# Placing the routing weights of eight tokens at once, in front of two expert tiles, in a hybrid mixer and PEER kernel

## The reference

```python
def one_block(xb):
    q = (xb @ w_q).reshape(tb, PEER_HEADS, 2, PEER_KEY_DIM)
    sc = jnp.einsum('thpk,hpnk->thpn', q, sub_keys).astype(jnp.float32)
    s1, i1 = lax.top_k(sc[:, :, 0], PEER_TOPK)
    s2, i2 = lax.top_k(sc[:, :, 1], PEER_TOPK)
    ...
    top_s, pos = lax.top_k(cand, PEER_TOPK)
    idx = jnp.take_along_axis(cidx, pos, axis=-1)
    gw = jax.nn.softmax(top_s, axis=-1).astype(xb.dtype)
    act = jax.nn.gelu(jnp.einsum('td,thkd->thk', xb, u[idx]), approximate=False)
    return jnp.einsum('thk,thkd->td', act * gw, v[idx])
```

## Time and profile before

| | |
|---|---|
| time, median of 3 runs | 1962.33 us (1962.28 to 1962.42) |
| span of the profiled execution | 1961.0 us |
| PE busy, share of the span | 1935.7 us, 99% |
| DVE, ACT, POOL busy | 60%, 49%, 63% |
| the stage of the last 64 up tiles | 217.1 us in each of the two layers |

### The profile page before, as it was taken

The page is one execution under the profiler, slowest core; times in us unless marked ns, Lnnn a source line. Parts: engine busy times, 40 slices in busy tenths (PEclk is TensorE's granted clock), DMA queues, the critical chain, the costliest instruction groups (busy, mean ns, idle before and its releaser), DMA issues.

```text
span 1961.0 us, 39380 instructions
## 1 busy us (share of the span) xinstructions
PE 1935.7 (99%) x13126; PEld 1750.7 (89%) x13126; DVE 1186.3 (60%) x2802; ACT 961.2 (49%) x1521; POOL 1242.2 (63%) x624
## 2 busy tenths in 40 slices
PE   9999999999999999999999999999999999999998
PEld 9888899899999888888898889998999998888886
DVE  4654499368898444444456536983688974444444
ACT  5644445444444444444555544454444444444444
POOL 6446688877776555555474476888777765555553
PEclk9999999999999999999999999999999999999999
DMA  6524555554444666655545245555444445555553
GB/s 217 179 91 145 187 182 176 190 172 156 155 155 156 196 193 192 195 192 194 187 142 185 87 152 186 183 181 189 165 157 152 158 163 192 195 193 193 192 192 135
DMA packets 93245, 338.48 MB, mean 173 GB/s; under 512 B 10353, under 2 KB 10737, under 8 KB 93169
## 3 DMA queue, kind: packets, MB, share of 16 engines
q1 hardware_dynamic: 93168, 337.54, 51.4%
HBM read 336.45 MB, written 1.05 MB: 172 GB/s over the span
## 4 chain that ended last, share of the span: by engine, by line
PE 95%; DVE 2%; ACT 1%; DMA 1%; issue 0%; SPq 0%; DVEq 0%
PE PS L1011 35%; PE PS L934 11%; PE PS L935 10%; PE PS L939 10%; PE PS L896 8%; PE PS L574 6%; PE PS L901 4%; PE PS L948 3%; PE PS L835 2%; DMA ring<-stream 1%; PE PS L559 1%; PE PS L541 1%; PE PS L564 1%; PE PS L560 1%; PE PS L613 1%; PE PS L921 0%
## 5 line engine op out<-in xcount | busy, mean ns | idle before, releaser
L478 POOL TENSOR_TENSOR WL<-ring,WH 128x1024 fp32r<-128x1024 f32 x360 | 867.8, 2412 | 383.0 <-ACT WH L1265 198.4
L1265 ACT CAST WH<-ring 128x1024 fp32r<-128x1024 f32 x512 | 538.2, 1051 | 753.5 <-PE PS L1011 329.7
L508 POOL TENSOR_TENSOR HX<-G,HX 128x256 fp32r<-128x256 f32 x256 | 372.2, 1454 | 320.2 <-ACT HX L1389 320.2
L1938 DVE TENSOR_TENSOR WL<-ring,WH 128x1024 fp32r<-128x1024 f32 x248 | 303.9, 1225 | 370.9 <-ACT WH L1265 370.9
L1011 PE MATMUL PS<-WH,HX 128*128 128x512 f32 x2048 | 506.4, 389 | 0.0
L1011 PEld LDWEIGHTS PS<-WH,HX 128*128 128x128 f32 x2048 | 384.2, 188 | 80.0 <-POOL HX L508 0.5
L934 PE MATMUL PS<-HX,WH 128*128 128x256 f32 x1664 | 418.1, 289 | 0.0
L935 PE MATMUL PS<-HX,WH 128*128 128x256 f32 x1664 | 407.7, 283 | 0.0
L935 PEld LDWEIGHTS PS<-HX,WH 128*128 128x128 f32 x1664 | 319.0, 192 | 0.0
L934 PEld LDWEIGHTS PS<-HX,WH 128*128 128x128 f32 x1664 | 317.9, 191 | 0.0
L1011 PE MATMUL PS<-WL,HX 128*128 128x512 f32 x1024 | 274.0, 389 | 0.0
(11 more groups left out here) (244 smaller groups left out, 1877.6 us busy)
## 6 DMA issues: line engine op xcount, KB each, us to landing
ring<-stream SPq DMA_DIRECT2D x636, 512.0 KB, 3.3
X<-x_t SPq DMA_DIRECT2D x4, 256.0 KB, 3.6
out_t<-X SPq DMA_DIRECT2D x2, 512.0 KB, 2.7
CN<-consts SPq DMA_DIRECT2D x1, 851.0 KB, 9.4
WF<-last SPq DMA_DIRECT2D x1, 512.0 KB, 10.1
PR<-params SPq DMA_DIRECT2D x2, 239.0 KB, 4.5
CN<-consts SPq DMA_DIRECT2D x1, 64.0 KB, 4.0
```

The source lines that it names most:

```text
L478: nc.gpsimd.tensor_tensor(WL[:, b, :], ring[:, slot, :], WH[:, b, :].bitcast(F32), ALU.subtract).then_inc(done, 1)
L508: nc.gpsimd.tensor_tensor(GL[:, s, :], G[:, tile, :], GH[:, s, :].bitcast(F32), ALU.subtract).then_inc(L.gl_ready, 1)
L1265: nc.scalar.copy(WH[:, b, :], ring[:, slot, :]).then_inc(L.hi_ready, 1)
L1938: V.tensor_tensor(WL[:, s % 2, :], ring[:, (U0 + s) % SLOTS, :], WH[:, s % 2, :].bitcast(F32), ALU.subtract).then_inc(L.vlo_ready, 1)
```

## The change

`place` of two groups is run in a row, in front of two up tiles, where each had stood in front of its own tile. The waits of both stand ahead of the first one. Since four groups of one-hots are now alive at once, their slots grow from 8 to 16; the second eight lie in SQ, a tile that has other uses only outside the expert layer. DVE makes four groups of one-hots ahead instead of two, and then runs two `weigh`, two `one_hot` and one `weigh_pair` in turn. ACT's order is as it was.

```diff
-        O2 = OH[:, :, 0:OW]
-        O1 = OH[:, :, OW:OW + 2 * P]
+        OHX = SQ[:, :, :].rearrange("p t n -> p (t n)").bitcast(F16)[:, 0:8 * (OW + 2 * P)].rearrange(
+            "p (s n) -> p s n", s=8)
+        O2 = [OH[:, k, 0:OW] for k in range(8)] + [OHX[:, k, 0:OW] for k in range(8)]
...
                         for i in range(4):
-                            o = bank[6 + g][:, i * P:(i + 1) * P]
+                            o = bank[6 + g % 2][:, i * P:(i + 1) * P]
...
-                    for s in range(SLOTS):
-                        if s % 2 == 0:
-                            pe.wait_ge(L.folded, N_WIDE - 1 + s // 2)
-                        pe.wait_ge(L.o_ready, s + 1)
-                        if s >= 2:
-                            pe.wait_ge(L.w_used, s - 1)
-                        place(s % 2)
-                        experts_in(s, HK + s + 1)
+                    for s in range(0, SLOTS, 2):
+                        pe.wait_ge(L.folded, N_WIDE - 1 + s // 2)
+                        pe.wait_ge(L.o_ready, s + 2)
+                        if s:
+                            pe.wait_ge(L.w_used, s)
+                        for e in range(2):
+                            place(s + e)
+                        for e in range(2):
+                            experts_in(s + e, HK + s + e + 1)
                     with pe.Fori(1, HK // SLOTS) as r:
-                        for s in range(SLOTS):
-                            if s % 2 == 0:
-                                pe.wait_ge(L.gelu_done, r * 2 + (HK // 2 + s // 2 - 1))
-                            pe.wait_ge(L.o_ready, r * SLOTS + (s + 1))
-                            pe.wait_ge(L.w_used, r * SLOTS + (s - 1))
-                            place(s % 2)
-                            experts_in(s, r * SLOTS + (HK + s + 1))
+                        for s in range(0, SLOTS, 2):
+                            pe.wait_ge(L.gelu_done, r * 2 + (HK // 2 + s // 2 - 1))
+                            pe.wait_ge(L.o_ready, r * SLOTS + (s + 2))
+                            pe.wait_ge(L.w_used, r * SLOTS + s)
+                            for e in range(2):
+                                place(s + e)
+                            for e in range(2):
+                                experts_in(s + e, r * SLOTS + (HK + s + e + 1))
...
                     one_hot(0)
+                    one_hot(1)
                     for k in range(SLOTS * TURN_ROUND + 4, SLOTS * TURN_ROUND + 8):
                         fold(k)
-                    one_hot(1)
+                    one_hot(2)
+                    one_hot(3)
...
-                    for g in range(GROUPS):
-                        weigh(g)
-                        if g + 2 < GROUPS:
-                            one_hot(g + 2)
-                        if g % 2 == 1 and g >= 5:
-                            weigh_pair((g - 5) // 2)
+                    for q in range(GROUPS // 2):
+                        weigh(2 * q)
+                        weigh(2 * q + 1)
+                        for g in (2 * q + 4, 2 * q + 5):
+                            if g < GROUPS:
+                                one_hot(g)
+                        if q >= 2:
+                            weigh_pair(q - 2)
```

More of the change, by code:

```diff
@@ L402, in program @@
         i_ps = PS[:, 3, 256:256 + 2 * P].rearrange("p (h e k) -> p e h k", h=HEADS, e=2)
-        O2 = OH[:, :, 0:OW]
-        O1 = OH[:, :, OW:OW + 2 * P]
+        OHX = SQ[:, :, :].rearrange("p t n -> p (t n)").bitcast(F16)[:, 0:8 * (OW + 2 * P)].rearrange(
+            "p (s n) -> p s n", s=8)
+        O2 = [OH[:, k, 0:OW] for k in range(8)] + [OHX[:, k, 0:OW] for k in range(8)]
+        O1 = [OH[:, k, OW:OW + 2 * P] for k in range(8)] + [OHX[:, k, OW:OW + 2 * P] for k in range(8)]
         iota3 = IOB[:, 0:3 * IW].rearrange("p (a b) -> p a b", a=3)
@@ L945, in place @@
                         for i in range(4):
-                            o = bank[6 + g][:, i * P:(i + 1) * P]
+                            o = bank[6 + g % 2][:, i * P:(i + 1) * P]
                             for a in range(2):
-                                mm = nc.tensor.matmul(o, O2[:, 4 * g + i, 0:P], O1[:, 4 * g + i, a * P:(a + 1) * P],
+                                mm = nc.tensor.matmul(o, O2[4 * g + i][:, 0:P], O1[4 * g + i][:, a * P:(a + 1) * P],
                                                       start=(a == 0), stop=(a == 1))
@@ L1875, in one_hot @@
                         for i in range(4):
-                            t, slot = 4 * g + i, g % 2 * 4 + i
-                            V.tensor_scalar(O2[:, slot, 0:3 * IC].rearrange("p (a b) -> p a b", a=3), iota3[:, :, 0:IC],
+                            t, slot = 4 * g + i, g % 4 * 4 + i
+                            V.tensor_scalar(O2[slot][:, 0:3 * IC].rearrange("p (a b) -> p a b", a=3), iota3[:, :, 0:IC],
                                             slotT[:, 1, t:t + 1], None, ALU.is_equal)
                             parts = PS[:, 2 + t // P, 0:2 * P].rearrange("p (a n) -> p a n", a=2)[:, :, t % P]
-                            ins = V.scalar_tensor_tensor(out=O1[:, slot, :].rearrange("p (a n) -> p a n", a=2),
+                            ins = V.scalar_tensor_tensor(out=O1[slot].rearrange("p (a n) -> p a n", a=2),
                                                          in0=bc(iota1, 1, 2), scalar=slotT[:, 0, t:t + 1],
```

## The result

The changed kernel takes 1999.18 us (1998.5 to 1999.67, 5 runs) against 1962.33 (1961.52 to 1962.99, 5 runs): 1.0186 times as long, 95% interval 1.0174 to 1.0197. The forecast was 1999.7, in a range of 1993.5 to 2009.5. The profiled span grew from 1961.0 to 1997.8 us, by 36.8.

A forecast was written before the change was run, and what follows sets the result against it. TensorE, busy for 99% of the span at full clock, was taken to bound the kernel. A wait of +40.9 us and a saving of -3.5 gave 1962.33 + 37.4 = 1999.7 us, range 1993.5 to 2009.5.

The forecast's parts named there:

- The wait: At 62 pair borders TensorE waits for keep(odd): 0.52 + 0.14 us each, 40.9 us in all (36.0 to 47.1).
- The release: From the end of ACT's keep to TensorE's matmul start: 0.14 us taken, with 0.06 and 0.24 as other values.
- the lower bound: Lowest size of the wait at the 62 pair borders: 62 x 0.58 = 36.0 us.
- The saving: Sixteen f16 matmuls in a row halve the changes of kind: 0.055 us per pair, -3.5 us (-4.5 to 0).
- its best pace: Second eight f16 matmuls of a pair at 0.44 us, a little under the mean, which saves 0.07 us.
- The sum: Wait plus saving over the span: +40.9 - 3.5 = +37.4 us, giving 1999.7 us.
- Everything behind the wait moves along: Placings, tiles and other engines' work shift by the same 0.66 us, so the wait returns at every border.
- DVE's order: Costs nothing: one-hots made for the pair after next have a whole pair's cover; without it, 2.3 us per late group.
- The sixteen matmuls kept their pace: Rival: the second eight f16 matmuls go 0.097 us apart, +17 us in place of -3.5, 2020 us; 5%.
- The granted clock was 1.00 in both stages: Rival: pauses lower TensorE's clock, up to +200 us a layer, from 2050 us on; 2%.
- The first rival: keep(odd) ends before the lowers do, so only the saving is left: 1958.8 us, at best 1957.8; 5%.

The follow-up runs named there:

- The wait alone: Kernel before, unpaired, with TensorE waiting in front of an even group for keep of the odd group just before it: 2003.41 us against 1962.52.
- The two parts measured alone: Kernel before with only the later bank wait: 2003.41 us; changed kernel with keep(odd) ahead of the second tile's cast: 1958.29 us; both against 1962.52.
- the 30 borders that were changed: Changed kernel, with one-hot and activation waits moved ahead of the tile before for each loop body's second pair: 1996.65 us against 1962.61.

## Why the prediction was right

- *The wait.* Forecast 62 x (0.52 + 0.14) = 40.9 us. The wait alone measured 2003.41 - 1962.52 = 40.9, and the idle time with its correction gives 41.3. The 0.52, the mean by which `keep` ends too late, was read from rows in which that hurt nobody: the end of `keep` against the start of the *next* placing, which was no wait at the time.
- *The release.* 0.14 us was taken from ACT's other release against 0.06 from DVE's, on the ground that the engines are the same. The size was right and the ground was not: ACT too releases TensorE in 0.05 to 0.06 us, where the bank's wait is the only one at the placing. By the program the matmul of the earlier trace rows also stands behind two waits (the landing of its piece and the emptied bank), which may be why its 0.14 fitted; no run tests that. That the right size came from a wrong ground is luck. With 0.06 the wait would have been the 36.0 us of the lower bound, and the forecast 1994.8.
- *The saving.* Forecast 0.055 us a pair, 3.5 us; measured 0.063 a pair, 4.0 to 4.2 us. This is the one term that was mis-sized, and inside its bounds. The prediction's own working gives 0.51 - 8 x 0.057 = 0.05 us; the 0.055 that it took lies between this and the 0.07 of its best pace, and no row gives it. With the 0.056 of a run of sixteen it is 0.51 - 8 x 0.056 = 0.06, which agrees with the 0.063 as far as starts rounded to 0.01 us can tell.
- *The sum.* The two parts measured alone give 40.9 - 4.2 = 36.7 us; the change itself measured 36.85.
- *Everything behind the wait moves along.* 62 waits at 62 borders show it. Their idle time shrinks from 0.60 to 0.41 us, as the lateness of `keep` in the rows of before does, from 0.62 to 0.41.
- *DVE's order* cost nothing, as forecast. But the reason was half wrong: the prediction said that without the cover of a whole pair, each late group would cost 2.3 us. With eight slots there is no such cover, and still only one border a layer waits, for 0.36 us. DVE makes both groups within the pair; late in the stage it ends 0.18 us before the placing starts.
- *The rivals.* The bank was not free in time. The sixteen matmuls kept their pace. The granted clock was 1.00 in both stages, through 62 pauses of 0.57 to 0.76 us (the idle time with its 0.16).
- *Slips that nothing hangs on.* The weight load of 0.097 us is 0.096 in the earlier trace rows. A pair of the changed kernel lasts 235.28 / 32 = 7.35 us on the mean, where the prediction had some 7.2 in one place and 7.4 in another.

The first rival, that the bank is free in time, named the cure: with `keep` ahead of the cast, the bank is free in time, and the kernel takes 1958.3 us where 1958.8 was worked out.

## What to carry to other kernels

The lesson is drawn from this one kernel. When two steps that alternate between two buffers are joined, the second buffer's wait comes earlier by a whole step. Before joining them, read in the trace when that buffer comes free, although nobody waits for it yet, and see what stands ahead of the freeing instruction on its own engine. If that is work which waits for the end of the present step, move the freeing instruction ahead of it; and let each wait stand only in front of what needs it.

## What was not expected of the hardware

TensorE was released by the same kind of ACT instruction in 0.15 us where the placing had other waits beside that for the bank, though these had long been met, and in 0.05 to 0.06 where it had that one alone. Over the 30 borders that were changed the idle time in brackets fell from 31.4 to 28.8 us, 0.09 us each. The times agree: 1999.18 - 1996.65 = 2.5 us, or 2.8 with each against the kernel before in its own session. The Trainium skill, page "Perfetto Trace Analysis", section "Identifying Dependency Chains", says that an instruction that waits on several engines may have some of its waits put into instructions of their own ahead of it. That fits, but the runs show only the durations.
